# An index, pool and convolution stage reordered: index sums by bank, pool's projection in the top-k, GpSimd taps, no zero products

## The chip, the cores and the metric
One core of a Trainium2 chip runs the whole program. The metric is the device time of one execution in microseconds (us), as the median of three executions. Engines: TensorE (PE in the rows, PEld its weight loads), VectorE (DVE), ScalarE (ACT), GpSimd (POOL), SyncE (SP, which issues the loads).

## The reference
Two transformer blocks, each of two layers, on one sequence of 256 tokens of width 1024, all in float32. The change touches the second block's layers, and one step of every layer. What a layer of the second block computes:
```python
u = rmsnorm(h) @ w_in        # q, k, v, index queries (16 heads of 64), index key, head weights, conv, pool
dots = einsum('bthd,bsd->bths', qi, ki)
idx = einsum('bths,bth->bts', relu(dots), wi) * scale       # causal; the 64 best keys of each row are kept
y_attn = softmax(q k^T on the kept keys) v                  # 8 heads
y_conv = silu(layernorm(depthwise_conv_31_taps(a * sigmoid(g)))) @ conv_pw
y_pool = (window sums of 2, 4, 8, 16 over their counts, minus u_pool) @ pool_w * pool_scale
h += rmsnorm(concat(y_attn, y_conv, y_pool) @ w_out)
h += rmsnorm(square(relu(rmsnorm(h) @ w_up)) @ w_down)
h += sigmoid(h @ ple_gate) * (p @ ple_proj)
```

## The kernel before, in words
Activations lie transposed, features on partitions. Every float32 product is made of three matmuls of rounded parts: upper by upper, upper by lower, lower by upper (`product`, L1988 to L1990). Weights come in chunks of up to 1 MB (128 x 2048), in one order for the whole program. SyncE loads chunk n into one of 3 raw buffers once the lower part of chunk n - 3 is made (L627, L628). ScalarE makes the upper part (`split_hi`, L788) once TensorE has released the ring slot of chunk n - 4, VectorE the lower one (`split_lo`, L1297). `next_hi(here, c)` and `next_lo(here, c)` split chunk c + 3. Each engine runs its own list, written out by hand, in order; engines meet at semaphores, so an engine that waits holds all that is listed behind it. Products go to one of 4 PSUM banks called `work` ("units", taken in turn) or to the four banks of `acc`.

The second block's layer, with its chunk numbers: 0 and 1 hold the last index queries, key and head weights, 2 and 3 the convolution's halves; then index queries ("qi", 1) to ("qi", 3), pool (`P2`), keys and values (`KV2`), queries (`Q2`, two chunks: 9 and 10), `WO2_POOL` 11, `WO2_LOW` 12, `WO2_HIGH` 13 (rows of w_out for pool and for the attention's two halves), `PW2` 14 (conv_pw, 256 KB), `WO2_CONV` 15, and from 16 the MLP's. Its order:
- `by_token` makes a chunk of index queries; VectorE applies the rotary part (`rope_unit`, L1695 to L1699), ScalarE scales the rows (`rows_of`, L1048), TensorE flips them (`turned`, L2118), ScalarE and VectorE split them (`index_queries`); `dots(c)` makes 4 heads of products against the keys in banks 1 to 3 of `acc`; ScalarE's `relus(c)` (L1054) and VectorE's `weighted(c)` (L1729) sum them into `idx`. Before, `weighted` waits for all three banks and frees them together (L1731), and pool's projection is cut in halves between the chunks.
- The top-k: VectorE takes 8 maxima and replaces them, 8 rounds (L1815, L1818), with rope and lower parts of queries and keys between the rounds; then a mask (L1835, L1838).
- The convolution: of 30 taps ScalarE multiplies each (`two_taps`, L1068, two instructions a tap) into one of three buffers, for which it waits until the tap three before is added, and GpSimd adds it (L735); after 8 taps GpSimd makes pool's window sums (L750 to L763), then the other taps.
- Eight heads in a relay: scores (TensorE), mask and maximum (L1395, L1399, VectorE), exp (L1155, ScalarE), flips of the probabilities (L2118), their upper (L836) and lower parts (L1310), product with the values; between them banks of w_out's products. In head 6 the conv's mean is summed (L2425, behind GpSimd's last tap); then variance, standard deviation (L1196), silu and `PW2`, in layer 0 also the first block's final norm (VectorE).
- The mix: w_out's conv rows (`WO2_CONV`) end the four banks; ScalarE loads the square root's table (L812) and squares each bank (L1215), TensorE sums the squares (`summed_by_bank`, L2058), VectorE normalises (L1893, L1900).
- The zero products: `open_acc` (L2076) writes zeros into all banks of `acc` with 8 matmuls before the first product of a sum, in three places in each layer of the first block and one in each of the second.

Of the kernel before, what the change touches and what calls it, by code (L numbers as in the profile page):

```python
# [40 lines left out]
P = 128  # L41
T = 256
# [35 lines left out]
TAPS_FIRST = 8  # L78
# [106 lines left out]
QK2, A2, G2_IN, P2, KV2, Q2, PW2, M2 = 0, 2, 3, 5, 8, 9, 14, 16  # L185
QI2 = (None, 4, 6, 7)
# [110 lines left out]
def build(nc, ins, out):  # L297
    with ExitStack() as ctx:
# [180 lines left out]
        part_2 = ["poolw", "kit", ("qit", 0), ("qit", 1), ("qit", 2), ("qit", 3), "v", "kd", "kt", ("qt", 0), ("qt", 1), "pooly"]  # L479
# [26 lines left out]
        taps_made = Signal(semaphore("taps_made"), 0, CONV_K2 - 1)  # L506
# [30 lines left out]
        def release(here, c):  # L537
# [37 lines left out]
            names = [("qk", 1), ("qk", 1), "a", "g", ("qi", 1), "pool", ("qi", 2), ("qi", 3), "kv", ("q", 0), ("q", 1)]  # L575
# [122 lines left out]
        def _(gp):  # L698
# [28 lines left out]
            for layer in range(DEPTH):  # L727
# [3 lines left out]
                def tap(j):  # L731
                    gp.wait_ge(*taps_made.at(here, j - 1))
# [37 lines left out]
        def _(act):  # L770
# [266 lines left out]
            for layer in range(DEPTH):  # L1037
# [107 lines left out]
                two_taps()  # L1145
# [24 lines left out]
                for hd in range(HEADS):  # L1170
# [14 lines left out]
                    if hd in (2, 3, 4):  # L1185
                        two_taps()
# [86 lines left out]
        def _(v):  # L1273
# [414 lines left out]
            for layer in range(DEPTH):  # L1688
# [93 lines left out]
                if layer == 0:  # L1782
                    v.wait_ge(*sum_ready.at(here, "pre"))
# [814 lines left out]
```

## Time and profile before
| | |
|---|---|
| median of 3 runs (2030.09 to 2030.71) | 2030.7 us |
| the profiled execution, its own time | 2032.99 us |
| its span | 2031.2 us |
| mean granted TensorE clock | 0.978 of full |

The span is what the profile's rows cover, from the first instruction to the last; the execution's own time has 1.8 us more. A row of a timeline is: start, duration, engine, line, operation, output and inputs by name, shapes, count; in brackets the engine's idle time before it and what ended it. Times are us from the span's start.

### The profile page before, as it was taken

What the parts mean: (1) busy time and instruction counts of PE and PEld (TensorE: products, weight loads), DVE (VectorE), ACT (ScalarE), POOL (GpSimd) and SP (SyncE); (2) the same over time, 40 slices, a digit from 0 to 9 for tenths busy, and PEclk for the clock granted to TensorE, in tenths of its full rate; (3) what the DMA queues carried; (4) which work ended last, traced back from release to release, by engine and by line L of the source; (5) the groups of instructions that cost most, each with busy time, mean ns of one, the idle gap of its engine ahead of it and who ended that gap; (6) DMA issues with size and microseconds to landing.
All of it is one profiled execution on the core that took longest, in us unless ns stands there. A gap on an engine that the chain in (4) does not pass through costs nothing.

```text
span 2031.2 us, 36691 instructions
## 1 busy us (share of the span) xinstructions
PE 1941.6 (96%) x15928; PEld 1923.0 (95%) x15928; DVE 1339.2 (66%) x1605; ACT 1011.4 (50%) x1271; POOL 214.6 (11%) x148
## 2 busy tenths in 40 slices
PE   7999999999999999999999999978999998789998
PEld 7999999999999999999999998968999998789998
DVE  6655777765558555787775557676756676666555
ACT  5433555554437444455554446766433475753333
POOL 3000100010002000100010002351100026410000
PEclk9999999999999999999999999969999998799999
DMA  7555454455554555544555554404354552225551
GB/s 260 181 186 185 143 169 157 146 197 186 187 184 156 198 187 189 178 154 132 166 175 179 187 187 145 158 27 146 126 203 170 173 174 89 84 85 203 191 183 67
DMA packets 246532, 329.55 MB, mean 162 GB/s; under 512 B 6247, under 2 KB 218789, under 8 KB 246373
## 3 DMA queue, kind: packets, MB, share of 16 engines
q1 hardware_dynamic: 246018, 326.79, 48.5%
q8 instruction: 126, 2.06, 0.4%
q0 software_dynamic: 96, 0.26, 0.0%
q10 hardware_dynamic: 258, 0.16, 0.0%
q14 instruction: 34, 0.27, 0.0%
HBM read 326.14 MB, written 1.05 MB: 161 GB/s over the span
## 4 chain that ended last, share of the span: by engine, by line
PE 80%; DVE 11%; ACT 6%; issue 1%; DMA 1%; POOL 0%; DVEq 0%; ACTq 0%; POOLq 0%; SPq 0%
PE work L1988 17%; PE work L1989 17%; PE work L1990 17%; PE acc L1988 9%; PE acc L1990 8%; PE acc L1989 8%; DVE w_lo L1297 3%; ACT w_hi L788 2%; ACT cs L1068 1%; DVE fa L1729 1%; PE work L2118 1%; DVE ra L1310 1%; DVE fa L1342 1%; PE acc L2058 1%; ACT fa L1068 0%
## 5 line engine op out<-in xcount | busy, mean ns | idle before, releaser
L1988 PE MATMUL work<-xh,w_hi 128*128 128x256 f32 x2560 | 723.1, 282 | 23.9 <-DVE xl L1331 12.8
L1297 DVE TENSOR_TENSOR w_lo<-raw,w_hi 128x2048 fp32r<-128x2048 f32 (+2 forms) x314 | 703.5, 2251 | 60.3 <-ACT w_hi L788 57.7
L1989 PE MATMUL work<-xl,w_hi 128*128 128x256 f32 x2560 | 720.8, 282 | 0.0
L1990 PE MATMUL work<-xh,w_lo 128*128 128x256 f32 x2560 | 719.1, 281 | 0.0
L788 ACT ACTIVATE w_hi<-raw 128x2048 fp32r<-128x2048 f32 (+2 forms) x314 | 578.2, 1849 | 171.2 <-PE work L1990 84.9
L1988 PEld LDWEIGHTS work<-xh,w_hi 128*128 128x128 f32 x2560 | 484.8, 189 | 27.7 <-issue 23.8
L1989 PEld LDWEIGHTS work<-xl,w_hi 128*128 128x128 f32 x2560 | 485.6, 190 | 0.2
L1990 PEld LDWEIGHTS work<-xh,w_lo 128*128 128x128 f32 x2560 | 485.4, 190 | 0.0
L1342 DVE TENSOR_TENSOR fa<-work,rstd 128x512 f32<-128x512 f32 x168 | 115.1, 689 | 403.4 <-PE work L1990 402.8
L1988 PE MATMUL acc<-ra,w_hi 128*128 128x256 f32 x1344 | 377.9, 281 | 0.0
L1990 PE MATMUL acc<-ra,w_lo 128*128 128x256 f32 x1344 | 377.5, 281 | 0.0
L1989 PE MATMUL acc<-ra,w_hi 128*128 128x256 f32 x1344 | 376.6, 280 | 0.0
L1989 PEld LDWEIGHTS acc<-ra,w_hi 128*128 128x128 f32 x1344 | 254.0, 189 | 0.0
L1990 PEld LDWEIGHTS acc<-ra,w_lo 128*128 128x128 f32 x1344 | 253.2, 188 | 0.0
L1988 PEld LDWEIGHTS acc<-ra,w_hi 128*128 128x128 f32 x1344 | 252.8, 188 | 0.0
L715 POOL TENSOR_TENSOR fa<-fa 128x512 f32<-128x512 f32 x36 | 70.4, 1954 | 1489.8 <-DVE xl L1331 849.0
L1988 PE MATMUL work<-ra,w_hi 128*128 128x256 f32 x624 | 177.8, 285 | 8.9 <-DVE w_lo L1297 3.9
L1989 PE MATMUL work<-ra,w_hi 128*128 128x256 f32 x624 | 176.6, 283 | 0.0
L1990 PE MATMUL work<-ra,w_lo 128*128 128x256 f32 x624 | 176.5, 283 | 0.0
L1988 PEld LDWEIGHTS work<-ra,w_hi 128*128 128x128 f32 x624 | 119.2, 191 | 10.0 <-issue 9.9
L1989 PEld LDWEIGHTS work<-ra,w_hi 128*128 128x128 f32 x624 | 119.3, 191 | 0.1
L1990 PEld LDWEIGHTS work<-ra,w_lo 128*128 128x128 f32 x624 | 119.3, 191 | 0.0
(289 smaller groups left out, 2308.1 us busy)
## 6 DMA issues: line engine op xcount, KB each, us to landing
raw<-in_ffn_w_gu_dram SPq DMA_DIRECT2D x88, 1024.0 KB, 5.1
raw<-in_w_in_dram SPq DMA_DIRECT2D x52, 1024.0 KB, 5.4
raw<-in_ffn_w_down_dram SPq DMA_DIRECT2D x44, 1024.0 KB, 5.1
raw<-in_w_up_dram SPq DMA_DIRECT2D x32, 1024.0 KB, 5.5
raw<-in_w_down_dram SPq DMA_DIRECT2D x32, 1024.0 KB, 6.9
raw<-in_w_mla_out_dram SPq DMA_DIRECT2D x8, 1024.0 KB, 5.6
raw<-in_w_o_dram SPq DMA_DIRECT2D x8, 1024.0 KB, 5.4
raw<-in_w_ple_gate_dram SPq DMA_DIRECT2D x8, 1024.0 KB, 5.3
```

The source lines that it names most:

```text
L715: gp.tensor_tensor(sq[:, 0:2, :], sq[:, 0:2, :], sq[:, 2 * b:2 * b + 2, :], ALU.add).then_inc(fold_step.sem, 1)
L788: act.activation(w_hi[:, s, 0:tiles * cols], raw[:, r, 0:tiles * cols], ACT.Copy).then_inc(hi_done.sem, 1)
L1068: last = act.activation(taps[(j - 1) % 3][:, k, :], yp[:, k, j:j + T], ACT.Copy, scale=column(here, V2_DW + 2 * j + k))
L1297: v.tensor_tensor(w_lo[:, s, 0:n], raw[:, r, 0:n], w_hi[:, s, 0:n].bitcast(F32), ALU.subtract).then_inc(lo_done.sem, 1)
L1310: v.tensor_tensor(dst, src, hi.bitcast(F32), ALU.subtract).then_inc(unit_taken.of(unit), 1)
L1342: v.tensor_tensor(dst, bank2(unit), over(scale_row, 2), ALU.mult).then_inc(unit_taken.of(unit), 1)
L1729: last = v.scalar_tensor_tensor(dst, src, wi[:, tb, hd:hd + 1], dst, ALU.mult, ALU.add)
L1988: pe.matmul(dst, ah, bh, start=start and i == 0, stop=False, skip_group_check=not group)
L1989: pe.matmul(dst, ah, bl, start=False, stop=False, skip_group_check=not group)
L1990: last = pe.matmul(dst, al, bh, start=False, stop=stop and i == len(pairs) - 1, skip_group_check=not group)
L2058: last = pe.matmul(dst, ones, src[:, k, :], start=k == 0, stop=k == KD - 1)
L2118: return pe.transpose(dst, src, ident)
```

## The change
It has five parts. (1) `weighted` waits for, sums and frees each bank by itself. (2) Pool's projection goes behind the last dots, in one piece, and VectorE takes it in the top-k's first round; in the first layer the sums of squares for the final norm go behind the last dots too; the work between the top-k's rounds goes to later rounds, the lower parts of the queries behind the top-k. (3) GpSimd multiplies every third tap itself (10 of 30) and makes pool's sums after 12 taps. (4) `open_acc` makes no products: the first product of each bank opens it (`first=`). (5) The lower parts of chunks 11 to 15 are made later: 11 in head 1, 12 and 13 in heads 3 and 4, 14 in head 5, 15 behind the conv branch, with its upper part; pool's rows of w_out are added in heads 2 to 5; `WO2_HIGH` is cut in two around `PW2`; the squares of the mix are summed between the banks of `WO2_CONV`.

The diff, cut to what is spoken of (12 columns of indent taken off):
```diff
@@ -75,7 +75,8 @@
-TAPS_FIRST = 8
+TAPS_FIRST = 12
+OWN_TAP = 3
@@ -141,7 +142,7 @@
-out += [("w_in_2", 0, KD, at, 256) for at in (IN2_A, IN2_G, IN2_QI, IN2_P, IN2_QI + 256, IN2_QI + 512, IN2_KV,
+out += [("w_in_2", 0, KD, at, 256) for at in (IN2_A, IN2_G, IN2_QI, IN2_QI + 256, IN2_QI + 512, IN2_KV, IN2_P,
@@ -182,8 +183,8 @@
-QK2, A2, G2_IN, P2, KV2, Q2, PW2, M2 = 0, 2, 3, 5, 8, 9, 14, 16
-QI2 = (None, 4, 6, 7)
+QK2, A2, G2_IN, KV2, P2, Q2, PW2, M2 = 0, 2, 3, 7, 8, 9, 14, 16
+QI2 = (None, 4, 5, 6)
@@ -729,7 +731,13 @@
-        gp.wait_ge(*taps_made.at(here, j - 1))
+        if j % OWN_TAP == 0:
+            weight = vecs[:, ALL.index(here), V2_DW + 2 * j:V2_DW + 2 * j + 2]
+            weight = weight.rearrange("p (a o) -> p a o", o=1).to_broadcast([P, 2, T])
+            gp.tensor_tensor(taps[(j - 1) % 3], yp[:, :, j:j + T], weight, ALU.mult).then_inc(own_tap.sem, 1)
+            gp.wait_ge(*own_tap.at(here, j // OWN_TAP - 1))
+        else:
+            gp.wait_ge(*taps_made.at(here, j - 1 - j // OWN_TAP))
@@ -1053,13 +1061,11 @@
-    taps_so_far = []
-    def two_taps():
-        for i in range(2):
-            j = len(taps_so_far) + 1
-            taps_so_far.append(j)
+    taps_left = [j for j in range(1, CONV_K2) if j % OWN_TAP]
+    def some_taps(n):
+        for j in [taps_left.pop(0) for _ in range(n)]:
@@ -1091,30 +1097,25 @@
-    next_hi(here, QI2[1])
+    some_taps(2)
...
-    next_hi(here, P2)
...
-    two_taps()
-    two_taps()
+    next_hi(here, QI2[1])
+    some_taps(2)
...
-    two_taps()
...
+    index_queries(2)
...
-    index_queries(2)
-    if layer == 0:
-        make_std(here, "pre", row=1)
-    two_taps()
-    next_hi(here, QI2[3])
+    some_taps(2)
...
-    next_hi(here, KV2)
...
-    two_taps()
+    next_hi(here, QI2[3])
+    next_hi(here, KV2)
@@ -1128,26 +1129,26 @@
-    two_taps()
+    next_hi(here, P2)
+    some_taps(2)
+    if layer == 0:
+        make_std(here, "pre", row=1)
+    some_taps(2)
...
+    rows_of(("q", 0), "q0", 0)
...
-    rows_of(("q", 0), "q0", 0)
-    two_taps()
-    two_taps()
+    some_taps(2)
...
-    two_taps()
+    preload(ACT.Exp)
+    act.wait_ge(*pooled.at(here, 0))
+    act.activation(pyh, py, ACT.Copy).then_inc(part_hi.event(here, "pooly"), 1)
+    some_taps(1)
...
-    two_taps()
-    preload(ACT.Exp)
-    act.wait_ge(*pooled.at(here, 0))
-    act.activation(pyh, py, ACT.Copy).then_inc(part_hi.event(here, "pooly"), 1)
-    two_taps()
-    two_taps()
@@ -1182,15 +1184,14 @@
-        if hd in (2, 3, 4):
-            two_taps()
+        if 0 < hd < 6:
+            some_taps(1)
...
-            next_hi(here, WO2_LOW)
...
-    assert len(taps_so_far) == CONV_K2 - 1
+    assert not taps_left
@@ -1205,8 +1206,9 @@
     last.then_inc(act_out.event(here, "lsilu"), 1)
     act.wait_ge(*act_out.at(here, "lsilu"))
     act.activation(lyh, ln_s, ACT.Copy).then_inc(part_hi.event(here, "ly"), 1)
+    next_hi(here, WO2_LOW)
+    hi_of_unit(here, U2["pw"], "pw", xh[:, 4:6, :], bank2(U2["pw"]))
     next_hi(here, WO2_HIGH)
-    hi_of_unit(here, U2["pw"], "pw", xh[:, 4:6, :], bank2(U2["pw"]))
     next_hi(here, PW2)
     next_hi(here, WO2_CONV)
     preload(ACT.Sqrt)
@@ -1717,18 +1719,18 @@
-        v.wait_ge(*relu_done.at(here, 3 * c + 2))
-        for g in range(4):
-            hd = INDEX_HEADS[c] + g
-            late, early = acc[:, 1 + g // 2, g % 2 * T:g % 2 * T + T], acc[:, 3, g * P:g * P + P]
-            parts = ((1, idx[:, P:384], late), (0, idx[:, 0:P], early))
-            for tb, dst, src in parts:
-                if (c, g) == (0, 0):
+        for i in range(3):
+            v.wait_ge(*relu_done.at(here, 3 * c + i))
+            n, dst, tb = (T, idx[:, P:384], 1) if i < 2 else (P, idx[:, 0:P], 0)
+            for g in range(512 // n):
+                hd = INDEX_HEADS[c] + (2 * i if i < 2 else 0) + g
+                src = acc[:, 1 + i, g * n:g * n + n]
+                if c == 0 and g == 0 and i != 1:
...
-            chain(here, last)
-        v.sem_inc(dot_taken.sem, 3)
+                chain(here, last)
+            v.sem_inc(dot_taken.sem, 1)
@@ -1772,26 +1774,13 @@
-    rope_unit(("qi", 1), 1)
-    next_lo(here, QI2[1])
-    index_queries(1)
-    weighted(0)
-    next_lo(here, P2)
-    rope_unit(("qi", 2), 2)
-    if layer == 0:
-        v.wait_ge(*sum_ready.at(here, "pre"))
-    scaled(here, U2["pool"], pu[:, :, POOL_PAD:])
-    index_queries(2)
-    next_lo(here, QI2[2])
-    weighted(1)
-    rope_unit(("qi", 3), 3)
-    next_lo(here, QI2[3])
+    for c in range(1, 4):
+        rope_unit(("qi", c), c)
+        weighted(c - 1)
+        index_queries(c)
+        next_lo(here, QI2[c])
+    rope_unit("kv", "kv", 2)
...
-    index_queries(3)
-    rope_unit("kv", "kv", 2)
-    weighted(2)
@@ -1816,17 +1805,16 @@
-        if r == 1:
+        if r == 0:
+            if layer == 0:
+                v.wait_ge(*sum_ready.at(here, "pre"))
+            scaled(here, U2["pool"], pu[:, :, POOL_PAD:])
+        if r == 3:
...
-        if r == 2:
+        if r == 5:
...
-        if r == 4:
+        if r == 7:
...
-        if r == 6:
-            queries_lo(0)
-        if r == 0 and layer == 0:
-            v.wait_ge(*std_ready.at(here, "pre"))
-            v.reciprocal(rstd[:, 1, :], std[:, 1, :]).then_inc(rstd_ready.event(here, "pre"), 1)
@@ -1859,14 +1848,17 @@
                 v.scalar_tensor_tensor(xl[:, 6 + k, :], bank(u)[:, 0:T], column(here, V2_PS + k),
                                        xh[:, 6 + k, :].bitcast(F32), ALU.mult, ALU.subtract).then_inc(unit_taken.of(u), 1)
         if hd == 1:
+            next_lo(here, P2)
+        if hd == 2 and layer == 0:
+            v.wait_ge(*std_ready.at(here, "pre"))
+            v.reciprocal(rstd[:, 1, :], std[:, 1, :]).then_inc(rstd_ready.event(here, "pre"), 1)
+        if hd == 3:
             next_lo(here, Q2)
-        if hd == 2:
+        if hd == 4:
             next_lo(here, Q2 + 1)
-        if hd == 3:
-            next_lo(here, WO2_POOL)
         if hd == 5:
             lo_of_unit(here, U2["ota"], "ota", xl[:, 0:2, :], bank2(U2["ota"]), xh[:, 0:2, :])
-            next_lo(here, WO2_LOW)
+            next_lo(here, WO2_POOL)
         if hd == 6:
             ready(here, U2["mean"])
             v.scalar_tensor_tensor(ln_t, over(bank(U2["mean"])[:, 0:T], 2), -1.0 / 256, cacc, ALU.mult, ALU.add).then_inc(
@@ -1881,8 +1873,9 @@
     lo_part(here, "ly", lyl, ln_s, lyh)
     if layer == 0:
         final_norm()
+    next_lo(here, WO2_LOW)
+    lo_of_unit(here, U2["pw"], "pw", xl[:, 4:6, :], bank2(U2["pw"]), xh[:, 4:6, :])
     next_lo(here, WO2_HIGH)
-    lo_of_unit(here, U2["pw"], "pw", xl[:, 4:6, :], bank2(U2["pw"]), xh[:, 4:6, :])
     next_lo(here, PW2)
     next_lo(here, WO2_CONV)
@@ -2068,12 +2061,9 @@
-def open_acc(here, name):
+def acc_free(here, name):
...
-    for b in range(NB):
-        for a in range(2):
-            pe.matmul(acc[:, b, a * T:a * T + T], zero_r[:, :], rot_r[:, :, :], start=True, stop=True)
@@ -2106,9 +2096,9 @@
-            open_acc(here, name)
+            acc_free(here, name)
...
-        accumulate(here, f + 3 * j + 1, hidden((j - 1) % 2))
+        accumulate(here, f + 3 * j + 1, hidden((j - 1) % 2), first=j == 1)
@@ -2333,7 +2323,7 @@
-                pe.wait_ge(*dot_taken.at(here, 3 * c - 1))
+                pe.wait_ge(*dot_taken.at(here, 3 * (c - 1) + i))
@@ -2347,38 +2337,18 @@
-    def pool_half(m):
-        if m == 0:
-            free(here, U2["pool"])
-        w = weights(here, P2)
-        last = product(bank2(U2["pool"])[:, m, :], [(columns(w, k * 256 + m * P), tiles((xh, xl), everything, k, everything))
-                                                    for k in range(KD)])
-        if m:
-            last.then_inc(unit_ready.sem, 1)
-    by_token(QI2[1], ("qi", 1))
-    pool_half(0)
-    pe.wait_ge(*unit_taken.at(here, U2["kit"]))
-    dots(0)
+    for c in range(1, 4):
+        by_token(QI2[c], ("qi", c))
+        if c == 1:
+            pe.wait_ge(*unit_taken.at(here, U2["kit"]))
+        dots(c - 1)
+        pe.wait_ge(*unit_taken.at(here, U2["qi", c]))
+        turned(("qit", c), tm[:, c % 2, :, :])
+    by_token(KV2, "kv")
+    dots(3)
...
-    pe.wait_ge(*unit_taken.at(here, U2["qi", 1]))
-    turned(("qit", 1), tm[:, 1, :, :])
-    by_token(QI2[2], ("qi", 2))
-    pool_half(1)
-    dots(1)
-    pe.wait_ge(*unit_taken.at(here, U2["qi", 2]))
-    turned(("qit", 2), tm[:, 0, :, :])
-    by_token(QI2[3], ("qi", 3))
-    free(here, U2["kv"])
-    w = weights(here, KV2)
-    token_half(KV2, "kv", 0, w)
-    dots(2)
-    pe.wait_ge(*unit_taken.at(here, U2["qi", 3]))
-    turned(("qit", 3), tm[:, 1, :, :])
-    token_half(KV2, "kv", 1, w).then_inc(unit_ready.sem, 1)
-    dots(3)
+    project(here, P2, U2["pool"])
@@ -2439,12 +2409,12 @@
-        if 0 < hd < 5:
-            if hd == 1:
+        if 1 < hd < 6:
+            if hd == 2:
...
-            accumulate(here, WO2_POOL, rows(6), first=True, banks=(hd - 1,))
+            accumulate(here, WO2_POOL, rows(6), first=True, banks=(hd - 2,))
@@ -2472,21 +2442,34 @@
-    accumulate(here, WO2_HIGH, rows(2))
+    accumulate(here, WO2_HIGH, rows(2), banks=range(2))
...
+    accumulate(here, WO2_HIGH, rows(2), banks=range(2, NB))
...
-    accumulate(here, WO2_CONV, rows(4), done=0)
...
-    summed_by_bank(here, NB + 1, bank(U2["mix"])[:, 0:T], unit_ready.sem)
+    def mix_sum(b):
+        pe.wait_ge(*sq_ready.at(here, NB + 1 + b))
+        for k in (2 * b, 2 * b + 1):
+            last = pe.matmul(bank(U2["mix"])[:, 0:T], ones, sq[:, k, :], start=k == 0, stop=k == KD - 1,
+                             skip_group_check=True)
+        return last
+    for b in range(NB):
+        accumulate(here, WO2_CONV, rows(4), done=0, banks=(b,))
+        if b:
+            mix_sum(b - 1)
+    mix_sum(NB - 1).then_inc(unit_ready.sem, 1)
...
-            open_acc(here, "mlppre")
+            acc_free(here, "mlppre")
...
-        accumulate(here, down_chunk(j - 2), hidden(j % 2))
+        accumulate(here, down_chunk(j - 2), hidden(j % 2), first=j == 2)
...
```

## Rows read from the trace of the kernel before

**Rows 1.** the page's busy table: engine, busy us (share), instructions
```profile
PE 1941.6 (96%) x15928; PEld 1923.0 (95%) x15928; DVE 1339.2 (66%) x1605; ACT 1011.4 (50%) x1271; POOL 214.6 (11%) x148
```

**Rows 2.** the zero products; their place in the chain that ended last; VectorE there
```profile
L2076 PE MATMUL acc<-rot_r,zero_r x64: 274/283/283, 41.9 to 1825.5; 128*128 128x256 f32 x64
...
1444.00 0.95 PE acc L2076 x8
...
1441.39 0.69 DVE L1928 TENSOR_TENSOR ra<-fa,ra 128x512 fp32r<-128x512 f32 x1 [0.70 <-ACT ra L1231]
```

**Rows 3.** TensorE's waits (us in total, times, longest); its timeline, both layers
```profile
PE acc L1988 <- DVEq L1731: 11.3, 4, 4.1
...
1327.50 0.55 PE L1988 MATMUL acc<-ka,ra 128*128 128x256 f32 x1 [3.93 <-DVEq L1731]
...
1361.14 0.45 PE L2118 MATMUL work<-consts,fa 128*128 128x128 f32 x1 [4.17 <-ACT fa L1155]
...
1374.09 0.44 PE L2118 MATMUL work<-consts,fa 128*128 128x128 f32 x2
...
1390.66 0.68 PE L2425 MATMUL work<-fa,consts 128*128 128x256 f32 x2
...
1408.86 0.39 PE L1988 MATMUL acc<-xh,w_hi 128*128 128x256 f32 x1 [1.41 <-DVE xl L1310]
...
1741.93 0.45 PE L2118 MATMUL work<-consts,fa 128*128 128x128 f32 x1 [5.49 <-ACT fa L1155]
...
1752.87 0.44 PE L2118 MATMUL work<-consts,fa 128*128 128x128 f32 x2
```

**Rows 4.** stretches: busy PE, PEld, DVE, ACT, POOL; PE clock, DMA share, GB/s
```profile
1317.00:1335.00 18.00, 13.79 (x87) 13.65 (x88) 11.53 (x26) 10.83 (x23) 15.83 (x12) 0.74 0.30 105
1349.00:1370.00 21.00, 12.39 (x55) 11.38 (x56) 17.50 (x50) 14.44 (x39) 11.60 (x9) 0.51 0.00 1
```

**Rows 5.** GpSimd's timeline, layer 0: pool's chain and the last tap
```profile
1316.61 0.23 POOL L750 MEMSET fa<- 128x32 f32 x3
...
1318.04 2.87 POOL L760 TENSOR_TENSOR fa<-fa,consts 64x256 f32<-64x256 f32 x1
1320.99 3.03 POOL L757 TENSOR_TENSOR fa<-fa 128x512 f32<-128x512 f32 x1
1324.10 0.79 POOL L760 TENSOR_TENSOR fa<-fa,consts 64x256 f32<-64x256 f32 x1
1324.97 1.04 POOL L757 TENSOR_TENSOR fa<-fa 128x512 f32<-128x512 f32 x1
...
1329.04 1.27 POOL L763 TENSOR_TENSOR fa<-fa 128x512 f32<-128x512 f32 x1
...
1384.44 1.27 POOL L735 TENSOR_TENSOR fa<-fa 128x512 f32<-128x512 f32 x1
```

**Rows 6.** ScalarE: the page's group of upper parts; its timeline before the squares
```profile
L788 ACT ACTIVATE w_hi<-raw 128x2048 fp32r<-128x2048 f32 (+2 forms) x314 | 578.2, 1849 | 171.2 <-PE work L1990 84.9
...
1411.71 1.28 ACT L812 ACT_TABLE_LOAD   x1
...
1413.11 1.56 ACT L1215 ACTIVATE fa<-acc 128x512 f32<-128x512 f32 x3
```

**Rows 7.** loads: KB each, median us to landing; conv_pw's issues; VectorE before the first
```profile
raw<-in_w_up_dram SPq DMA_DIRECT2D x32, 1024.0 KB, 5.5
...
raw<-in_conv_pw_dram SPq DMA_DIRECT2D x2, 256.0 KB, 2.8
...
L628 SPq DMA_DIRECT2D raw<-in_conv_pw_dram x2: 368/368/368, 1323.2 to 1703.4; - x2
...
1320.83 2.29 DVE L1297 TENSOR_TENSOR w_lo<-raw,w_hi 128x2048 fp32r<-128x2048 f32 x1 [0.52 <-ACT w_hi L788]
```

**Rows 8.** VectorE's timeline: a lower part beside GpSimd's work
```profile
1300.29 3.34 DVE L1297 TENSOR_TENSOR w_lo<-raw,w_hi 128x2048 fp32r<-128x2048 f32 x1
```

**Rows 9.** the chain that ended last: the mix's sums of squares
```profile
1414.80 3.47 PE work L2058 x16
```

More of the change, by code:

```diff
@@ L226, in units_2 @@
     names = [("qk", 0), ("qk", 1), "a", "g", "kit", ("qit", 0)]
-    names += [("qi", 1), ("qit", 1), ("qi", 2), "pool", ("qit", 2), ("qi", 3), ("qit", 3), "kv"]
+    names += [("qi", 1), ("qit", 1), ("qi", 2), ("qit", 2), ("qi", 3), ("qit", 3), "kv", "pool"]
     names += [("q", 0), "kt", ("q", 1), ("qt", 0), ("qt", 1), ("sc", 0), ("sc", 1)]
@@ L478, in build @@
         part_1 += [("merged", b) for b in range(NB)] + ["p"]
-        part_2 = ["poolw", "kit", ("qit", 0), ("qit", 1), ("qit", 2), ("qit", 3), "v", "kd", "kt", ("qt", 0), ("qt", 1), "pooly"]
+        part_2 = ["poolw", "kit", ("qit", 0), ("qit", 1), ("qit", 2), ("qit", 3), "v", "kd", "kt", "pooly", ("qt", 0), ("qt", 1)]
         part_2 += [("pt", 0), "pool"] + [("pt", hd) for hd in range(1, 6)] + ["ota", ("pt", 6), ("pt", 7), "otb", "ly", "pw", "p"]
@@ L505, in build @@
         conv_done = Signal(semaphore("conv_done"), 0, 1)
-        taps_made = Signal(semaphore("taps_made"), 0, CONV_K2 - 1)
+        taps_made = Signal(semaphore("taps_made"), 0, CONV_K2 - 1 - (CONV_K2 - 1) // OWN_TAP)
+        own_tap = Signal(semaphore("own_tap"), 0, (CONV_K2 - 1) // OWN_TAP)
         tap_added = Signal(semaphore("tap_added"), 0, CONV_K2 - 1)
@@ L574, in release @@
                 return unit_ready, U1["gate"] + c - G1
-            names = [("qk", 1), ("qk", 1), "a", "g", ("qi", 1), "pool", ("qi", 2), ("qi", 3), "kv", ("q", 0), ("q", 1)]
+            names = [("qk", 1), ("qk", 1), "a", "g", ("qi", 1), ("qi", 2), ("qi", 3), "kv", "pool", ("q", 0), ("q", 1)]
             if c < WO2_POOL:
@@ L1177, in _ @@
                     if hd == 0:
+                        some_taps(2)
                         for k in range(2):
@@ L1843, in rinv @@
                         vec_out.event(here, ("rinv", hd)), 1)
+                queries_lo(0)
                 for hd in range(2):
                     masked_scores(here, U2["sc", hd], hd % 2, s2_sb, idx, SCALE2, hd)
+                queries_lo(1)
                 lo_part(here, "pooly", pyl, py, pyh)
-                queries_lo(1)
                 for hd in range(HEADS):
@@ L2243, in _ @@
                         if hp == 1:
-                            open_acc(here, "qkv")
+                            acc_free(here, "qkv")
                         pe.wait_ge(*unit_taken.at(here, UE["o", hp - 1]))
-                        accumulate(here, c + 3, (oh, ol))
+                        accumulate(here, c + 3, (oh, ol), first=hp == 1)
                     else:
```

## The prediction

> **What bounds the kernel now.** I read the page's busy table first: TensorE works through 96% of the span [rows 1], so only two things can shorten the run, matmuls that go away and the little idle time of TensorE. The zero products come first: 64 of them, eight in each of eight places [rows 2]. Then the waits of TensorE and its own timeline [rows 3]. In the first layer of the second block (call it layer 0; layer 1 repeats it) it stands before the index dots until VectorE has taken the scores (four times in the two layers, 11.3 us), 4.17 us before the first flip of probabilities, which waits for exp 0 behind the top-k (5.49 in layer 1), and 1.41 before the conv rows of w_out. [...] The reader should see that this stage is a relay of five engines: the end of each stretch is set by whichever message comes last.
>
> **Part A, no zero products.** In the chain of what ended last, eight of them take 0.95 us [rows 2]. What stands next, the hidden tile's lower part (L1928), is done at 1442.08, 1.8 us ahead of them [rows 2], so no wait takes their place there. 8 x 0.95 = **7.6 us gained**. Bounds: 4, if half the places wait, and 7.6.
>
> **Part B, index sums, pool and own taps up to the first exp.** I lay out the new order from the start of the second index queries (1280.42 in layer 0), at 0.12 us a matmul: 5.8 for a projection, 2.9 for a chunk's dots.
> - Dots 3 ended at 1332.8. Ahead of them go pool's projection (5.8), in layer 0 the sums of squares (as long as 16 matmuls in [rows 9], 3.5), the waits for VectorE, since a bank now needs only the same bank of the chunk before, and some 2.5 us of the lower clock. A wait of 1.8 us comes in behind dots 0, as the flips need the rows of ("qi", 1) and pool no longer covers them. Dots 3 end near 1318.2.
> - Behind them TensorE does the sums to 1321.7 and pool to 1327.5; VectorE, in round 0 of the top-k since about 1324, stands for pool until 1327.5 and again near 5 us for ("q", 0), all inside the time below. The top-k ends near 1344.
> - GpSimd begins its pool chain when pool is taken, 1328.2. Before, the chain ran from 1316.61 to 1330.3; 4.1 us of it are two operations of 2.87 and 3.03 where the next of the same kind took 0.79 and 1.04, with VectorE making w_lo beside them [rows 5, 7]. In the top-k no w_lo runs: 9.6 us, to 1337.9. Taps 13 and 14 are added at 39.3 and 40.7 (1.27 each and the gap).
> - ScalarE asks for tap 16 right behind the kt copies (1336), but that buffer is free only when tap 13 is added, and 17's when 14 is. **All of ScalarE is queued behind that**: w_hi 1.8 and table load 1.4 [rows 6], pool's copy, tap 19, then the queries' upper part until 1346.7 and the rows of ("q", 1) until 1347.5. TensorE flips and scores (lower clock) to 1349.5, VectorE masks, 1.2, exp 0.9, first flip at 1351.9 against 1361.14 [rows 3]: 9.2 gained.
> - Layer 1 has no sums of squares, but there tap 12 (behind ScalarE's 10 and 11, which follow dots 3) ends after pool is taken: chain start 1327.3 on the same scale, flip at 1350.9 where it stood at 1358.9: 8.0 gained.
> The 1.8 us wait may drop the clock; I take 0.9 a layer back. **Part B: -15.4 us**, bounds -24 (ScalarE not held) and -7 (the chain as slow as before).
>
> GpSimd's own multiply isn't in the trace. Nearest are its adds of the same 512 columns, 1.04 to 1.27 alone, 3.03 beside a w_lo [rows 5]; I take 1.28. [...]
>
> **Part C, the heads.** Chunk 11's lower part moves from before the top-k to head 1. With three raw buffers the load of chunk 14 is issued only then: before, chunk 11's w_lo ended at 1323.1, and conv_pw's load was issued at 1323.2 [rows 7]. ScalarE asks for chunk 14 in head 1 too. In times of before: it gets there at 1368.6, VectorE ends chunk 11 at 71.6, the load takes 2.8 [rows 7], so ScalarE stands until 74.5. Behind it are a w_hi, a tap and exp 3, and the flips of head 3 come at 76.8, where they came at 1374.09 [rows 3]: +2.7; in layer 1, where they came 10.9 us behind the first flip [rows 3] and not 12.9, +4.7. The later heads carry two w_lo more and, in layer 0, a reciprocal of 1.75. GpSimd has 11 adds and 4 own products left from tap 20 on, 15 x 1.41 = 21 us, plus about 2 for each of four w_lo that it meets, and tap 29 reaches it only in head 5, near 90. It ends near 96. The conv's mean (L2425) began at 1390.66, and GpSimd had been done since 1385.7 [rows 3, 5]. So it begins **5.3 us later in layer 0, 6.7 in layer 1**, with 1.4 more for the clock: **+13.4**. Bounds +2 and +20. The banks of w_out's pool rows, one head later, cost nothing: they fill the gaps of head 5.
>
> **Part D, the mix.** WO2_HIGH's second half covers the wait for pw, so WO2_CONV begins 0.8 us earlier in layer 0 and 1.3 in layer 1. But chunk 15's lower part moves behind the conv branch and, in layer 0, behind final_norm: it ends at 1407.4 instead of 1390. Only then is chunk 18 loaded (w_up, 5.5 us [rows 7]): ScalarE splits it from 1413.0 to 14.85, loads its table (1.4) and squares bank 0 from 1416.2, where it squared from 1413.11 [rows 6]. And TensorE now asks for square 0 **between** banks: it stands from 1411.0, then has 0.65 for the square, four sums of 0.87 and two banks of 1.46 to go, 7.1 us, to 1423.3. Before, the sums took 3.47 behind bank 3, to 1418.3 [rows 9]. +5.1 in layer 0; without final_norm, in layer 1, +3.0. Gaps of 5 and 4 us drop the clock, as that of 3.93 did [rows 4]; of the 6.4 us of work behind each I double some 2.7: +5.5. **Part D: +13.6**, bounds +1 and +18.
>
> Sum: -7.6 - 15.4 + 13.4 + 13.6 = **+4.0 us**. The profiled execution took 2033.0, its span and 1.8 around it, 2.3 more than the median of 2030.7; so 2037.0 for a profile and 2034.7 for a median. What a measurement of this kernel can tell from no change is about 0.2%, 4 us.
>
> **Rivals.**
> 1. *Chunks 14 and 18 land in time and hold nobody* (not slower). For it: the DMA share over 1349 to 1370 is 0.00 [rows 4], the queue is free; against it: the load is issued behind w_lo [rows 7]. Then part C is GpSimd's end alone (+2.4, +3.6, clock 1.4), part D 1.8 + 1.5: -12.3 us, 2018.4. Chance 0.30.
> 2. *GpSimd sets both ends* (slower still). For it: a w_lo took 3.34 us beside GpSimd against 2.29 alone [rows 7, 8], and GpSimd now has 40 operations a layer for the taps where it had 30. If the pool chain takes 13.7 us again, +4.1 a layer, and the mean waits 2 more a layer: +12.2 on the sum, 2047. It decides from the chain's length: past 9.6 us each microsecond goes to ScalarE. [...] The top-k's operations read one tile, so I leave the chain clean: chance 0.15.
> 3. *The zero products are gone, but TensorE waits as long*, for the hidden tile or w_lo. Against it the 1.8 us of part A. 2042. Chance 0.05.
> The forecast itself 0.50, its own range 2029 to 2041.
>
> **Numbers.** Faster (below 2026.6): nearly all of rival 1, 0.29. Same: half of the forecast, 0.25. Slower: the other half, rivals 2 and 3 and what is left, 0.46. Both signs hold much, so the range takes in both sides: 2016 to 2046 leaves out 2 in 10.
>
> **What would show it.** Part A: no L2076 rows. Part B: the first flip of exp 0 about 9 us nearer to the second index queries, ScalarE idle before tap 16 until GpSimd's add of tap 13. Part C: ScalarE waiting for DMA of conv_pw in head 1, and L2425 waiting for GpSimd. Part D: ScalarE waiting for in_w_up before the squares, TensorE idle 4 to 5 us inside the banks of WO2_CONV, a lower clock behind. If ScalarE isn't held in head 1 or before the squares, the forecast is wrong towards rival 1; if the pool chain is over 13 us, towards rival 2.

## The result, and the profile after

The changed kernel took **2038.0 us**, median of 7 runs (2037.25 to 2041.81), where the kernel before took 2030.7 (2029.07 to 2032.38, 7 runs beside it): a ratio of 1.0039, 95% interval 1.0027 to 1.0051, so 5.5 to 10.4 us slower. The ratio times 2030.7 gives +7.9; the forecast was +4.0: 2034.7, and 2037.0 for a profiled execution. The one profiled took 2041.8 (span 2039.9, 8.7 more than before's), the highest of the seven. The page's busy table of the kernel after, which answers to [rows 1]:

```profile
PE 1937.5 (95%) x15864; PEld 1916.8 (94%) x15864; DVE 1349.2 (66%) x1605; ACT 996.2 (49%) x1231; POOL 232.6 (11%) x168
```

64 matmuls fewer, 40 instructions moved out of ScalarE, 20 into GpSimd, and TensorE busy 4.1 us less; the span still grew. TensorE's timeline says where. I cut each layer of the second block at four marks: the start of the second index queries, the first flip of probabilities, the conv's mean, and the first matmul of the MLP's pair, which ends the mix. First the kernel before, as far as [rows 3] don't have it:

```profile
1280.42 0.36 PE L1988 MATMUL work<-w_hi,xh 128*128 128x256 f32 x1
...
1424.24 0.55 PE L1988 MATMUL work<-xh,w_hi 128*128 128x256 f32 x1 [5.99 <-DVE xl L1331]
...
1663.44 0.36 PE L1988 MATMUL work<-w_hi,xh 128*128 128x256 f32 x1
...
1769.67 2.05 PE L2425 MATMUL work<-fa,consts 128*128 128x256 f32 x4
...
1804.66 0.55 PE L1988 MATMUL work<-xh,w_hi 128*128 128x256 f32 x1 [5.99 <-DVE xl L1331]
```

Then TensorE's timeline of the kernel after; L2108 is the flip, L2395 the mean, L2456 the mix's sums of squares, L1981 the first product of a tile:

```profile
1274.25 0.36 PE L1981 MATMUL work<-w_hi,xh 128*128 128x256 f32 x1
...
1284.73 0.66 PE L2108 MATMUL work<-consts,fa 128*128 128x128 f32 x4 [1.86 <-ACT fa L1056]
...
1294.98 0.66 PE L2108 MATMUL work<-consts,fa 128*128 128x128 f32 x4 [1.20 <-ACT fa L1056]
...
1305.22 0.66 PE L2108 MATMUL work<-consts,fa 128*128 128x128 f32 x4 [1.21 <-ACT fa L1056]
...
1343.60 1.11 PE L2108 MATMUL work<-consts,fa 128*128 128x128 f32 x4 [7.94 <-ACT fa L1056]
...
1348.40 0.87 PE L2108 MATMUL work<-consts,fa 128*128 128x128 f32 x3 [1.13 <-ACT fa L1156]
...
1365.92 0.88 PE L2108 MATMUL work<-consts,fa 128*128 128x128 f32 x3 [3.29 <-ACT fa L1156]
...
1385.80 1.11 PE L2395 MATMUL work<-fa,consts 128*128 128x256 f32 x4
...
1412.12 2.07 PE L2456 MATMUL work<-fa,consts 128*128 128x256 f32 x4 [5.83 <-ACT fa L1217]
...
1426.64 0.55 PE L1981 MATMUL work<-xh,w_hi 128*128 128x256 f32 x1 [5.99 <-DVE xl L1333]
...
1664.89 0.36 PE L1981 MATMUL work<-w_hi,xh 128*128 128x256 f32 x1
...
1738.45 0.52 PE L2108 MATMUL work<-consts,fa 128*128 128x128 f32 x3 [1.20 <-ACT fa L1156]
...
1755.21 0.87 PE L2108 MATMUL work<-consts,fa 128*128 128x128 f32 x3 [2.46 <-ACT fa L1156]
...
1775.00 1.11 PE L2395 MATMUL work<-fa,consts 128*128 128x256 f32 x4
...
1799.13 2.08 PE L2456 MATMUL work<-fa,consts 128*128 128x256 f32 x4 [4.54 <-ACT fa L1217]
...
1814.68 0.55 PE L1981 MATMUL work<-xh,w_hi 128*128 128x256 f32 x1 [5.99 <-DVE xl L1333]
```

Subtracting neighbours gives the table (us, after minus before; "predicted" are the terms of the prediction):

```
stretch                          layer 0   layer 1   both    predicted
B start to first flip              -6.6      -4.9    -11.5   -15.4
C first flip to conv's mean        +7.9      +8.8    +16.7   +13.4
D conv's mean to MLP's pair        +7.3      +4.7    +12.0   +13.6
A everything else (the remainder)                     -8.5    -7.6
span                                                  +8.7    +4.0
```

Both layers lose 8.6 us between the first and the last mark; the zero products give about as much back as one layer loses. Three waits of ScalarE are behind C and D and part of B; its timeline, layer 0 of the kernel after:

```profile
1335.25 0.91 ACT L1074 ACTIVATE cs<-fa,vecs 128x256 f32<-128x256 f32 x2 [2.71 <-POOL fa L743]
1336.66 0.91 ACT L1074 ACTIVATE cs<-fa,vecs 128x256 f32<-128x256 f32 x2 [0.50 <-POOL fa L743]
...
1363.47 0.63 ACT L796 ACTIVATE w_hi<-raw 128x512 fp32r<-128x512 f32 x1 [6.39 <-DMA raw<-in_conv_pw_dram]
...
1408.16 1.91 ACT L796 ACTIVATE w_hi<-raw 128x2048 fp32r<-128x2048 f32 x1 [3.58 <-DMA raw<-in_w_up_dram]
```

The DMA queue's own timeline shows that chunk 14's load is issued when VectorE is through with chunk 11 (1356.39 + 2.28):

```profile
1358.77 0.37 SPq L630 DMA_DIRECT2D raw<-in_conv_pw_dram  x1
```

And in the DMA view over 1340 to 1380 us (KB, median us to landing) it takes 4.7 us, where it took 2.8 before [rows 7]. In layer 0 that is bad luck of this one execution: in the trace of a kernel with the same heads it took 2.6 (One wait for three banks, below).

```profile
raw<-in_conv_pw_dram SPq DMA_DIRECT2D x1, 256.0 KB, 4.7
```

The windows (start and end, length, busy PE, PEld, DVE, ACT, POOL; clock, DMA share, GB/s) show the granted clock. The first two rows are the kernel before's stretches C and D in layer 0, 0.79 and 0.95 of full clock:

```profile
1361.14:1390.66 29.52, 26.75 (x181) 25.66 (x182) 20.62 (x40) 19.84 (x62) 10.10 (x8) 0.79 0.33 108
1390.66:1424.24 33.58, 25.77 (x196) 24.38 (x195) 21.16 (x28) 19.98 (x33) 0.00 (x0) 0.95 0.38 126
```

The kernel after has 0.69 and 0.87 in the same two stretches, and 0.62 around the stall in head 1. Over B the clock rose, from 0.86 to 0.93 in layer 0 and from 0.85 to 0.91 in layer 1.

```profile
1348.40:1385.80 37.40, 31.75 (x182) 29.95 (x182) 23.32 (x43) 19.07 (x63) 20.39 (x15) 0.69 0.24 76
1385.80:1426.64 40.84, 28.00 (x196) 25.95 (x195) 23.28 (x29) 22.11 (x34) 0.00 (x0) 0.87 0.34 118
1357.00:1372.00 15.00, 11.41 (x58) 10.66 (x56) 8.54 (x13) 5.21 (x18) 4.82 (x4) 0.62 0.06 19
```

### The profile page after: what moved, and what is told of

Read it like the earlier page. It is cut to its first block, busy times and chain, and to the rows that moved or that the text cites. A ratio compares the mean times of both kernels' runs of the same rounds, so it can differ in the third digit from the quotient of the medians.

```text
span 2039.9 us, 36557 instructions
## 1 busy us (share of the span) xinstructions
PE 1937.5 (95%) x15864; PEld 1916.8 (94%) x15864; DVE 1349.2 (66%) x1605; ACT 996.2 (49%) x1231; POOL 232.6 (11%) x168
## 4 chain that ended last, share of the span: by engine, by line
PE 77%; DVE 12%; ACT 5%; issue 2%; POOL 2%; DMA 2%; ACTq 0%; DVEq 0%; POOLq 0%; SPq 0%
PE work L1981 17%; PE work L1982 17%; PE work L1983 17%; PE acc L1983 8%; PE acc L1981 8%; PE acc L1982 8%; DVE w_lo L1299 4%; ACT w_hi L796 2%; DVE fa L1731 1%; DVE fa L1344 1%; DVE ra L1312 1%; PE work L2108 1%; DMA raw<-in_w_up_dram 1%; PE acc L2051 1%; PE work L2456 1%
## 5 line engine op out<-in xcount | busy, mean ns | idle before, releaser
L1981 PE MATMUL work<-xh,w_hi 128*128 128x256 f32 x2560 | 723.2, 283 | 24.1 <-DVE xl L1333 12.8
L1981 PEld LDWEIGHTS work<-xh,w_hi 128*128 128x128 f32 x2560 | 484.5, 189 | 28.1 <-issue 24.0
L1981 PE MATMUL acc<-ra,w_hi 128*128 128x256 f32 x1344 | 377.8, 281 | 0.0
L1981 PEld LDWEIGHTS acc<-ra,w_hi 128*128 128x128 f32 x1344 | 252.8, 188 | 0.0
L1981 PE MATMUL work<-ra,w_hi 128*128 128x256 f32 x624 | 177.9, 285 | 8.9 <-DVE w_lo L1299 3.9
L1981 PEld LDWEIGHTS work<-ra,w_hi 128*128 128x128 f32 x624 | 119.2, 191 | 10.1 <-issue 9.9
```

The lines of the kernel that those rows point to most:

```text
L1981: pe.matmul(dst, ah, bh, start=start and i == 0, stop=False, skip_group_check=not group)
```

## The experiments

Differences from the changed kernel are taken as differences of the two ratios to the kernel before, times 2030.7; each ratio's interval is 2 to 3 us to either side, so that such a difference is known to some 3 or 4 us.

**Part A alone.** In the kernel before:

```
- open_acc(here, name)
+ acc_free(here, name)
- accumulate(..., hidden(...))
+ accumulate(..., hidden(...), first=j == 1)
```

> The kernel before with part A alone: the zero products leave, the first product of each accumulation opens its region. Theory (part A as predicted): 8 places of 0.95 us on the path, -7.6 us, 2023.1. Rival 3 of the prediction (TensorE waits as long for the hidden tile or w_lo): within 2 us of the kernel before. A part in between would mean that some of the eight places wait, at 0.95 us each.

2025.1 us, ratio 0.9972 (0.9964 to 0.9981): **-5.7**, between 3.9 and 7.3. The 7.6 is just outside; the size was a little too large, the sign and mechanism hold, and rival 3 falls. The six places ahead of layer 0's first mark bring it 5.4 us forward in this kernel's trace (1280.42 to 1275.01) and 6.17 in the changed kernel's (to 1274.25).

**Chunk 11's lower part early.** In the changed kernel:

```
  queries_lo(0)
+ next_lo(here, P2)
  ...
- if hd == 1:
-     next_lo(here, P2)
```

> The changed kernel, with chunk 11's lower part between the first queries' lower part and the first masking (VectorE idles 2.41 us there) and no longer in head 1. Theory (part C: the load of chunk 14 comes behind it and holds ScalarE in head 1 by 6.39 us in layer 0 and 8.2 in layer 1): the load is issued near 1346 us, ScalarE waits for no conv_pw, the flips of head 3 come 4.6 and 5.8 us nearer to the first flip, some of the lower clock behind goes: -13 us against the changed kernel, 2025, bounds -9 and -16. Rival (GpSimd's last tap sets the conv's mean; it ended 0.8 us before the mean): the heads get faster but TensorE then waits for GpSimd before the mean, and no more than 4 us are gained.

2027.7, ratio 0.9988 (0.9979 to 0.9996): **-10.4** from the changed kernel. In this kernel's timeline (DMA queue, ScalarE, TensorE) the load goes out 12.1 us earlier, ScalarE's split of chunk 14 has no wait, the mean comes at 1378.56 instead of 1385.80.

```profile
1346.65 0.37 SPq L630 DMA_DIRECT2D raw<-in_conv_pw_dram  x1
...
1356.55 0.63 ACT L796 ACTIVATE w_hi<-raw 128x512 fp32r<-128x512 f32 x1
...
1378.56 1.11 PE L2394 MATMUL work<-fa,consts 128*128 128x256 f32 x4
...
1761.10 1.13 PE L2394 MATMUL work<-fa,consts 128*128 128x256 f32 x4 [0.88 <-POOL fa L743]
```

Of the 7.2 us by which this mean is earlier, about half is the slow load of the changed kernel's trace. Measured against a second trace of that kernel, with the faster load in layer 0 (One wait for three banks, below), from each layer's first mark to the mean, chunk 11 early gains 3.5 us in layer 0 and 7.2 in layer 1, 10.7 together, about the 10.4 that the runs give.

So the load was the bound, not GpSimd: even with the heads this much faster GpSimd's last tap holds the mean 0.88 us in layer 1 only. In the changed kernel it had idled 9.15 us for one of ScalarE's taps, so it was late because ScalarE was.

**The mix: chunk 15 early, the sums behind, both.** The first moves both parts' splits from behind the conv branch (next_lo there goes likewise) to heads 5 and 6:

```
  hi_of_unit(here, U2["ota"], ...)
+ next_hi(here, WO2_LOW)
  ...
  if hd == 6:
+     next_lo(here, WO2_LOW)
      ready(here, U2["mean"])
  ...
- next_hi(here, WO2_LOW)
```

> The changed kernel, with chunk 15 split in heads 5 and 6 and no longer behind the conv branch; the sums of squares stay between the banks. Theory (part D: the late load of chunk 18 sets the first square, and the order of the sums makes TensorE wait for it): the square of bank 0 comes about 3.5 us earlier in layer 0 and 3 in layer 1, TensorE's wait inside the banks falls from 5.8 and 4.5 us to some 2: -8 us against the changed kernel with the clock, 2030. Rival (the order of the sums alone costs the time, ScalarE being held by its three splits and the table load anyway): less than 2 us gained.

and the second

```
  for b in range(NB):
      accumulate(here, WO2_CONV, rows(4), done=0, banks=(b,))
-     if b:
-         mix_sum(b - 1)
+ for b in range(NB - 1):
+     mix_sum(b)
```

> The changed kernel, with the mix's sums of squares behind all four banks as before; the loads stay as they are. Theory (both matter): TensorE does its banks until 1409 us in layer 0, the squares run from 1411.5 to 1414.2 and the sums end near 1415.5 instead of 1420.65; in layer 1 the like: -5 us a layer, -10 in all against the changed kernel, 2028. Rival (the late load alone costs the time, and the order of the sums is harmless): less than 2 us gained.

> The changed kernel with both mendings of the mix: chunk 15 split in heads 5 and 6, and the sums of squares behind the four banks. Theory (the two are one interlock, each alone left TensorE waiting 3.0 us for a square): with both, the banks run through, the squares are there by the time the banks end, and the sums end 4.6 us a layer earlier than with the early split alone: -15 us against the changed kernel, 2023; part D's term of the prediction was 13.6. Rival (they gain the same microseconds twice): as the better of the two, 2030.

Chunk 15 early: 2031.9, ratio 1.0003 (0.9993 to 1.0013), **-7.3**. Sums behind: 2030.3, 0.9999 (0.9990 to 1.0008), **-8.1**. Both: 2022.8, 0.9962 (0.9949 to 0.9974), **-15.6**. Neither rival stands: each mending gains alone and they add. The wait that took 5.8 us in the changed kernel, in TensorE's waits over layer 0 (us in total, times, longest), with chunk 15 early:

```profile
PE work L2456 <- ACT fa L1217: 3.0, 1, 3.0
```

and with both:

```profile
PE work L2456 <- ACT fa L1217: 0.2, 1, 0.2
```

With the sums behind it is 3.0 too (1.8 in layer 1), but once, with all banks done. This is an interlock: the square waits for ScalarE's queue, that for a load, that for VectorE, and the bank behind the square waits for all three.

**The taps on ScalarE later.**

```
- some_taps(2)
  next_hi(here, Q2 + 1)
  ...
- some_taps(1)
  for i in range(2):
      if i:
+         some_taps(2)
          rows_of(("q", 1), "q1", 1)
      hi_of_unit(here, U2["qt", i], ...)
+ some_taps(1)
```

> The changed kernel, with ScalarE's taps 16 and 17 behind the first queries' upper part and tap 19 behind the second's. Theory (ScalarE stands 3.2 us in layer 0 and 5.1 in layer 1 for a tap's buffer, and everything up to the first exp is queued behind it): no wait for GpSimd before the queries; the first flip of probabilities comes 1.8 us earlier in layer 0, where VectorE's top-k ends only 0.7 us before the queries' upper part, and 4.4 in layer 1: -6 us against the changed kernel, 2032. Rival (GpSimd sets both ends): its taps come no earlier, the conv's mean stays where it was and nothing is gained.

2036.1, ratio 1.0025 (1.0016 to 1.0034): **-2.8**, half of what the theory gave, and by the intervals alone not told apart from the rival's nothing. The steps in the trace do what was expected (TensorE's timeline of this kernel; the same two flips were at 1348.40 after a wait of 7.94 for the rows of q1, and the mean at 1385.80):

```profile
1339.61 0.73 PE L2108 MATMUL work<-consts,fa 128*128 128x128 f32 x4 [4.39 <-ACT fa L1056]
...
1346.77 0.88 PE L2108 MATMUL work<-consts,fa 128*128 128x128 f32 x3 [1.12 <-ACT fa L1156]
...
1381.44 1.11 PE L2395 MATMUL work<-fa,consts 128*128 128x256 f32 x4
```

From the layer's first mark the first flip comes 1.1 us earlier in layer 0 and 3.8 in layer 1. The 4.4 us at the mean of layer 0 say little: 3.7 of them are the changed kernel's slow load. Against the trace with the faster load (next run) the mean of layer 0, from the first mark, comes 0.2 us earlier, so there the rival is right: the heads give back what the flip gains. And this profile is the fastest of eleven runs (2030.7, the median 5.4 more), so the trace flatters the kernel. The runs settle the sign: all eleven (up to 2037.04) are faster than all seven of the changed kernel (from 2037.25), and than all four of the next one (from 2038.23), measured beside them. So the taps gain some 2 to 3 us, not 6.

**One wait for three banks.** `dot_taken.at(here, 3 * (c - 1) + i)` becomes `dot_taken.at(here, 3 * c - 1)`.

> The changed kernel, with TensorE waiting for all three banks of the chunk before, as in the kernel before, at every bank of the dots. Theory (what ended the 11.3 us of waits is the order on VectorE, the lower part of a chunk being behind the weighted sums; the last of them is done 1.9 us before the next dots begin): no difference, within 0.1%. Rival (the wait by bank is what gains, as the prediction's step had it): 1 to 3 us slower at six places, +6 us or more.

2038.4, ratio 1.0040 (1.0026 to 1.0054): **no difference**. VectorE's timeline of the changed kernel shows why: its last sums on dots 0 end at 1289.02, and dots 1 begin at 1290.90.

```profile
1279.65 2.32 DVE L1299 TENSOR_TENSOR w_lo<-raw,w_hi 128x2048 fp32r<-128x2048 f32 x1
1281.90 0.28 DVE L1697 TENSOR_TENSOR fa<-work,cols 128x128 f32<-128x128 f32 x1
...
1287.89 1.13 DVE L1731 SCALAR_TENSOR_TENSOR fa<-acc,cols,fa 128x128 f32<-128x128 f32 x3
```

As this edit changes nothing, its trace (span 2039.8) is a second trace of the changed kernel, and it shows how far one trace can be trusted. B is the same to 0.02 us in both layers. C is 33.7 us in layer 0 where the changed kernel's trace had 37.4 (37.3 and 36.6 in layer 1), and the kernel with the sums behind, which has the same heads, has 33.8. The load of chunk 14 took 2.6 us in layer 0 here. In this kernel's DMA view over 1340 to 1380 us, and in the timelines of ScalarE and TensorE:

```profile
raw<-in_conv_pw_dram SPq DMA_DIRECT2D x1, 256.0 KB, 2.6
...
1361.21 0.63 ACT L796 ACTIVATE w_hi<-raw 128x512 fp32r<-128x512 f32 x1 [6.05 <-DMA raw<-in_conv_pw_dram]
...
1382.68 1.11 PE L2395 MATMUL work<-fa,consts 128*128 128x256 f32 x4
```

D is 43.1 instead of 40.8 in layer 0, where ScalarE waits 5.11 us for w_up and not 3.58. By this trace the table's rows would read B -11.5, C +13.8, D +14.2 and A -7.8. So the table knows B well, and C and D to some 2 to 4 us only.

**The rope ahead of the lower part.** The same rows show the next thing: TensorE is through with the second queries at 1280.17, but their rope (L1697) starts at 1281.90, behind a lower part. So

```
- next_lo(here, G2_IN)
  for c in range(1, 4):
      rope_unit(("qi", c), c)
+     next_lo(here, QI2[c - 1] if c > 1 else G2_IN)
      weighted(c - 1)
      index_queries(c)
-     next_lo(here, QI2[c])
  rope_unit("kv", "kv", 2)
+ next_lo(here, QI2[3])
```

> The changed kernel, with each chunk's lower part on VectorE behind the rope of the next index queries and no longer ahead of it. Theory (the flips behind dots 0, 1 and 2 wait 1.86, 1.20 and 1.21 us in layer 0 for the rows of the next queries, which follow VectorE's rope, and that stands behind a lower part until 1.7 us after TensorE is through; the prediction had only the first of the three waits): the waits nearly go, 4 us a layer, and dots 3 and the first flip come that much earlier: -7 us against the changed kernel, 2031. Rival (the wait moves: the lower part now delays the weighted sums and the next dots wait for VectorE): within 2 us.

2030.4, ratio 1.0002 (0.9994 to 1.0011): **-7.5**. From the first mark to the first flip it is 4.1 us less than in the changed kernel in layer 0 and 3.8 in layer 1. Of the waits of 1.86, 1.20 and 1.21 nothing is left in TensorE's waits over 1265 to 1325 us, whose only row is

```profile
PE acc L1981 <- DVE ra L1312: 0.3, 1, 0.3
```

**No taps of GpSimd's own.** `OWN_TAP = 31`, and ScalarE makes three taps where it made two (two for one in heads 1 and 2, and before the queries).

> The changed kernel, with all thirty taps multiplied by ScalarE, three where it made two; GpSimd only adds. Theory (ScalarE is held by the free buffer of tap 13's add and by the load of chunk 14, not by the count of its taps; GpSimd has slack before the conv's mean): within 3 us of the changed kernel, as the ten taps of 0.9 us a layer that ScalarE takes back lie mostly in its idle time. Rival (the third of the taps is what the change gains in the first flip and the heads): +6 us or more.

2043.0, ratio 1.0073 (1.0059 to 1.0087): **+6.9**, so the rival's number, and my theory falls. ScalarE's timeline of this kernel, layer 0: it now stands for three buffers in a row.

```profile
1334.85 0.91 ACT L1074 ACTIVATE cs<-fa,vecs 128x256 f32<-128x256 f32 x2 [2.73 <-POOL fa L743]
1336.26 0.91 ACT L1074 ACTIVATE cs<-fa,vecs 128x256 f32<-128x256 f32 x2 [0.50 <-POOL fa L743]
1337.67 0.91 ACT L1074 ACTIVATE fa<-fa,vecs 128x256 f32<-128x256 f32 x2 [0.51 <-POOL fa L743]
```

From the first mark the first flip comes 2.2 us later in layer 0 than in the changed kernel, and 1.3 in layer 1. The profiled span is no longer than the changed kernel's (2039.9 both), but that trace has the slow loads, and here chunk 14's load took 2.5 and 2.4 us. Against the rope-first kernel, which has the changed kernel's heads and loads of 2.7, C is 1.0 and 1.3 us longer. Together that is 5.9 of the 6.9 us; what in those heads costs it wasn't looked into.

**All four mendings, and with the rope first.** The changed kernel with chunk 11 early, chunk 15 early, the sums behind and the taps later:

> The changed kernel with all of it: chunk 11's lower part before the first masking, chunk 15 split in heads 5 and 6, the sums behind the banks, the three taps later. Theory (the costs stand one behind the other and add): -10 for chunk 11, -15 for the mix, -6 for the taps, less 3 where GpSimd's last tap comes to set the conv's mean: -28 against the changed kernel, 2010. Rival (GpSimd sets the conv's mean once ScalarE is free): chunk 11's and the taps' gain are not both had, 2018.

2008.2, ratio 0.9887 (0.9874 to 0.9901): **-30.9** from the changed kernel. The parts alone (-10.4, -15.6, -2.8) make -28.8, so they add as far as the intervals tell. And with the rope first:

> The kernel with all four mendings (it took 2008.2) and the rope ahead of the lower part. Theory: the same 7 us as in the changed kernel alone, as nothing else covers those waits: 2001. Rival (in layer 0 VectorE's top-k already sets the first flip, so what TensorE gains before it is given back there): 2005 to 2008.

**1999.2 us** (1997.87 to 2000.32), ratio 0.9851 (0.9838 to 0.9865): 30 us faster than the kernel before and 38 faster than the changed one; the rope's 7 us are had again. GpSimd now holds TensorE before the mean, 0.90 and 0.89 us in the two layers. TensorE's timeline of this kernel:

```profile
1343.29 0.88 PE L2107 MATMUL work<-consts,fa 128*128 128x128 f32 x3 [1.45 <-ACT fa L1156]
...
1372.55 1.13 PE L2394 MATMUL work<-fa,consts 128*128 128x256 f32 x4 [0.90 <-POOL fa L743]
```

## Why the prediction was right, and where its steps were off

The sign, the case (the forecast, not a rival) and the mechanisms held. The sum was too low by 3.9 us (+4.0 against the runs' +7.9), and by 4.7 on the profile (+8.7). The one term that is off in every trace is part B, by 3.9 us.

- **Part A**: -7.6 predicted, -5.7 measured alone, -8.5 and -7.8 as remainder in the two traces. Held, a little too large.
- **Part B**, -15.4 predicted, -11.5 found in both traces. Its chain of steps is right to the tenth where it was read from rows: the wait behind dots 0 (1.8 predicted, 1.86), the pool chain (9.6; 1324.39 to 1333.96 is 9.6), ScalarE held for taps 13 and 14. What failed is the step "a wait of 1.8 us comes in behind dots 0": there are three such waits, behind dots 1 and 2 too, 1.2 us each, because a w_lo stands ahead of each rope. That is 2.4 of the 2.7 us by which layer 0's first flip was later than laid out (74.15 us behind the mark instead of 71.5). The rope-first kernel shows that these waits are real time on the path. The other half of that step, that TensorE's wait by bank saves time, is wrong as well: with one wait for all three nothing changed. What took the 11.3 us of waits away is VectorE's side, where the weighted sums now stand ahead of the lower part; that VectorE also sums bank by bank wasn't undone by itself.
- **Part C**, +13.4 predicted, +16.7 and +13.8 found in the two traces, and -10.4 when only its load is mended. The wait was there, in head 1, for conv_pw, 6.39 us (6.05 in the other trace) where 5.9 were laid out. Measured from the first flip, the flips of head 3 come 4.6 and 5.8 us later than before in the two layers (1.8 and 6.6 in the other trace), where 2.7 and 4.7 were laid out. Held, within what one trace can tell: most of the +3.3 is the load that took 4.7 us in layer 0 of one execution instead of the 2.8 of [rows 7]. In layer 1 it took 4.7 in both traces, which the prediction didn't have. One step named the wrong cause: the mean did **not** wait for GpSimd. With the first flip put at before's 1361.14, GpSimd ended at 1397.7 (96 laid out) and the mean began at 1398.5: the slower heads put it there, and GpSimd, as the early-load kernel shows, moves with them. The two are close, though: in layer 0 of both kernels with the sums behind, GpSimd holds the mean by 0.6 us. That the sum of C came out right with GpSimd's end as its basis is in part luck.
- **Part D**, +13.6 predicted, +12.0 and +14.2 found. First square at 1411.49, TensorE standing 5.83 and 4.54 us inside the banks where 5 and 4 were foretold, and a granted clock of 0.87 and 0.88 over D where the kernel before had 0.95 and 0.94. Held. Undone it gives 15.6, more than it had cost, as D then is 32.4 us in both layers where the kernel before had 33.6 and 35.0.
- **The clock terms** (2.5 us of part B's gain and 0.9 a layer taken back, 1.4 in C, 5.5 in D) have work at the lower clock cost twice. No run shows any of them by itself. In windows of 1 us over B to D the granted clock is 0.50 or 1.00 of full, apart from those in which it changes; at 0.50 one 128x256 product of the kernel after starts 0.21 us behind the last (1414.21, 1414.42), at 1.00 it is 0.12 (1405.07, 1405.19). In B, layer 0, the kernel before has 0.50 from 1326 to 1335, around and behind its wait of 3.93 us, and the kernel after 1.00 in every window up to 1337. In C the kernel before has 0.79 and 0.87 in the two layers, the kernel after 0.69 and 0.72. In D, behind the waits of 5.83 and 4.54, the kernel after has 0.50 until about 1416.2 and 1805.3, over 4.1 and 6.2 us of work: by an estimate from these windows 5.1 us lost, near the 5.5.
- **Rival 1** (loads in time) needed a load issued before the heads: the trace and the chunk 11 run show that it wasn't. Chunk 11 early and chunk 15 early, with the order of the sums kept, are what it described; their two gains make -17.7 from the changed kernel, where it had -16.3 from the forecast. So its price was about right, and only its condition wasn't met. No kernel has just these two.
- **Rival 2** (GpSimd sets both ends): the chain took 9.6 us and not more, so it didn't decide. It comes next: in the last kernel GpSimd holds the mean by 0.9 us. That the top-k's operations would leave the chain alone was the author's estimate; beside them its operations of 128x512 took 1.04 to 1.29 us in both layers, where two operations beside a w_lo had taken 2.87 and 3.03 [rows 5].

GpSimd's own multiply took 1.04 us, not 1.28. GpSimd's timeline, kernel after: the pool chain's start, the multiply with the add behind it, and the last tap:

```profile
1324.39 0.24 POOL L758 MEMSET fa<- 128x32 f32 x3 [0.48 <-DVE fa L1344]
...
1336.58 1.04 POOL L737 TENSOR_TENSOR fa<-fa,vecs 128x512 f32<-128x512 f32 x1
1337.69 1.27 POOL L743 TENSOR_TENSOR fa<-fa 128x512 f32<-128x512 f32 x1
...
1383.72 1.27 POOL L743 TENSOR_TENSOR fa<-fa 128x512 f32<-128x512 f32 x1
```

## What to carry to other kernels

Moving the lower part of a weight chunk moves the **load of the chunk three places on** with it, and whatever engine splits that chunk; before moving such a step, look up which load its completion releases and who asks for it first, and put it where its engine idles anyway (2.4 us before the first masking, 3.7 before the mean). Don't let an in-order engine produce something that the next engine needs between two of its own steps unless it is certain to be on time: a sum between banks turned ScalarE's lateness into TensorE's. And when a wait shows up behind one step of a loop, ask at once whether it is behind all of them.

## What had not been expected of the hardware

- The same 256 KB load took 2.4 to 2.8 us to landing in 20 of the 26 times that the thirteen traces hold, and 4.1 to 4.8 us in six. All ten loads that were issued before the heads were fast; of the sixteen issued in head 1 the slow ones are both of the changed kernel's and layer 1's of four others, though the DMA share around the changed kernel's was 0.06. The cause is open.
- GpSimd's two-input operations of 512 columns took mostly either 1.04 us (the multiply by a weight per row, and three of pool's four window sums) or 1.27 to 1.29 (the taps' adds and the fourth window sum). What tells them apart wasn't looked into. Beside VectorE's w_lo the add took 3.1 to 3.2 us, near the 3.03 of [rows 5].
- Two profiled executions stood 4 and 5 us from their medians in opposite directions (the changed kernel +3.8, the taps kernel -5.4), as much as some of the effects looked for, and one stretch of two traces of the same code differed by 3.7. Ratios over many runs decided here, and traces only told where.
